# Layer 0 mixer: y projection and memory keys dealt over twelve steps of the dilated attention

## What is computed

```python
def lru_dilated_mixer(h, cos, sin, w_in, conv_w, conv_b, wa, ba, wx, bx, lam, w_out):
    proj = h @ w_in
    x_br, y_br, q, k, v = jnp.split(proj, list(AB_SPLITS), axis=-1)
    rec = rg_lru(causal_depthwise_conv(x_br, conv_w, conv_b), wa, ba, wx, bx, lam) * jax.nn.gelu(y_br)
    q = partial_rope(heads(q), cos, sin)
    k = partial_rope(heads(k), cos, sin)
    att = dilated_attention(q, k, heads(v)).transpose(0, 2, 1, 3).reshape(Bsz, L, B_WIDTH)
    return jnp.concatenate([rec, att], axis=-1) @ w_out
```

## Time and profile before

| | |
|---|---|
| three runs | 1431.32, 1430.82, 1430.17 us (median 1430.82) |
| profiled execution | 1429.49 us; its span in the trace is 1427.3 us, so 2.2 us lie around it |
| PE busy | 1360.2 us of the span (95%) |
| DVE, ACT, POOL busy | 778.0, 344.1, 314.9 us |
| mean granted TensorE clock | 0.979 of full speed |
| from the first y matmul to the first matmul of `xq0` | 156.05 to 336.13 us of the span |

### The profile page before, as it was taken

The page is one execution under the profiler, slowest core; times in us unless marked ns, Lnnn a source line. Parts: engine busy times, 40 slices in busy tenths (PEclk is TensorE's granted clock), DMA queues, the critical chain, the costliest instruction groups (busy, mean ns, idle before and its releaser), DMA issues.

```text
span 1427.3 us, 17280 instructions
## 1 busy us (share of the span) xinstructions
PE 1360.2 (95%) x6344; PEld 1107.2 (78%) x6344; DVE 778.0 (55%) x1159; ACT 344.1 (24%) x715; POOL 314.9 (22%) x358
## 2 busy tenths in 40 slices
PE   8999998899899999999999996799899999999997
PEld 7877785588677888888888884688678888888886
DVE  6997865336556443334436768537475443344434
ACT  4338134212332111001112235513331110001113
POOL 2221224221311121121212125312321212121120
PEclk9999999999999999999999998899999999999998
DMA  5322221023322322233232320022123332323221
GB/s 196 112 89 82 83 96 50 30 89 103 104 74 89 103 90 102 94 98 101 91 103 89 105 88 30 1 87 90 59 89 97 95 103 89 103 89 103 92 99 74
DMA packets 90241, 127.16 MB, mean 89 GB/s; under 512 B 5440, under 2 KB 53824, under 8 KB 90176
## 3 DMA queue, kind: packets, MB, share of 16 engines
q1 hardware_dynamic: 90176, 126.27, 27.6%
HBM read 124.15 MB, written 2.10 MB: 88 GB/s over the span
## 4 chain that ended last, share of the span: by engine, by line
PE 74%; DVE 14%; issue 5%; POOL 3%; DMA 2%; ACT 1%; SPq 0%; DVEq 0%; POOLq 0%; ACTq 0%
PE ps L489 23%; PE ps L493 23%; PE ps L492 23%; DVE w_lo L869 2%; PE ps L593 2%; DVE prob_attn L985 2%; DVE xc L1094 1%; POOL w_hi L452 1%; PE ps L627 1%; POOL prob_attn L444 1%; PE ps L610 1%; DVE acc L890 1%; DVE h L909 1%; POOL prob_xattn L444 1%; DMA raw<-in_xa_wkv 1%
## 5 line engine op out<-in xcount | busy, mean ns | idle before, releaser
L869 DVE TENSOR_TENSOR w_lo<-raw,w_hi 128x1024 fp32r<-128x1024 f32 x226 | 279.4, 1237 | 478.2 <-POOL w_hi L452 476.0
L452 POOL TENSOR_SCALAR w_hi<-raw 128x1024 fp32r<-128x1024 f32 x226 | 252.4, 1117 | 974.6 <-DMA raw<-in_w_gate_up 409.9
L489 PE MATMUL ps<-z_hi,w_hi 128*128 128x512 f32 x1040 | 408.7, 393 | 9.6 <-DVE w_lo L869 3.4
L492 PE MATMUL ps<-z_lo,w_hi 128*128 128x512 f32 x1040 | 405.3, 390 | 0.0
L493 PE MATMUL ps<-z_hi,w_lo 128*128 128x512 f32 x1040 | 405.3, 390 | 0.0
L489 PE MATMUL ps<-f_hi,w_hi 128*128 128x512 f32 x608 | 239.6, 394 | 0.9 <-issue 0.9
L493 PE MATMUL ps<-f_hi,w_lo 128*128 128x512 f32 x608 | 237.1, 390 | 0.0
L492 PE MATMUL ps<-f_lo,w_hi 128*128 128x512 f32 x608 | 237.0, 390 | 0.0
L489 PEld LDWEIGHTS ps<-z_hi,w_hi 128*128 128x128 f32 x1040 | 195.5, 188 | 53.4 <-DVE w_lo L869 4.2
L492 PEld LDWEIGHTS ps<-z_lo,w_hi 128*128 128x128 f32 x1040 | 195.7, 188 | 41.7 <-issue 1.4
L493 PEld LDWEIGHTS ps<-z_hi,w_lo 128*128 128x128 f32 x1040 | 195.6, 188 | 41.0
(11 more groups left out here) (188 smaller groups left out, 1194.5 us busy)
## 6 DMA issues: line engine op xcount, KB each, us to landing
raw<-in_w_gate_up SPq DMA_DIRECT2D x176, 256.0 KB
raw<-in_w_down SPq DMA_DIRECT2D x44, 512.0 KB
raw<-in_w_in SPq DMA_DIRECT2D x28, 512.0 KB
raw<-in_w_out SPq DMA_DIRECT2D x20, 512.0 KB
raw<-in_xa_wkv SPq DMA_DIRECT2D x16, 512.0 KB
raw<-in_xa_wq SPq DMA_DIRECT2D x8, 512.0 KB
raw<-in_xa_wo SPq DMA_DIRECT2D x8, 512.0 KB
raw<-in_w_qkv SPq DMA_DIRECT2D x8, 512.0 KB
```

Source lines behind the costliest of these rows:

```text
L452: pool.tensor_scalar(w_hi[:, slot], raw[:, slot], 1.0, 1.0, ALU.mult, ALU.mult).then_inc(s_hi, 1)
L489: ins = pe.matmul(o, whi, rhi, start=start, stop=False)
L492: pe.matmul(o, whi, rlo, start=False, stop=False)
L869: dve.tensor_tensor(w_lo[:, slot], raw[:, slot], w_hi[:, slot].bitcast(F32), ALU.subtract).then_inc(s_lo, 1)
```

## The change

The stages `in_y` and `attn0` become one stage `mixer` of twelve steps. A step s takes a third of one head pair: the scores of both heads of pair s // 3 for the blocks (128 and 256), 384 or 512 columns. Behind them on PE stands one unit of weights: a half of a pair of y tiles (`y_half`, steps 0 to 7), the memory keys (steps 8 to 11), and from step 12 on a unit of `out0`. The transposes run four steps behind the scores, two thirds of a head at a time, the products with v at steps 7, 10, 13 and 16. The y weights come as units of 512 rows by 256 columns. The scores of both heads of a pair use rows 0 to 63 and 64 to 127 of the array, alternating. `y_in` has two tiles in another place, probabilities and their transposes live where `lru_r`, `lru_a` and z were, the row order of `out0` is 4, 0, 1, 2, 3, 5 (in units of 256 rows; 4 and 5 hold the attention's output), and on DVE `qk_tile(6)` moves ahead of a `low_to`.

```diff
-          ("in_v", 1, 4), ("in_y", 2, 4), ("attn0", 2, 2), ("out0", 2, 6)]
+          ("in_v", 1, 4), ("mixer", 2, 6), ("out0", 2, 6)]
+OUT0_ROWS = (4, 0, 1, 2, 3, 5)
+STEPS, Y_UNITS = 12, 8
...
+        def turns_of(s):
+            if 4 <= s < STEPS + 4:
+                return [((s - 4) // 3, *divmod(k, 3)) for k in (2 * ((s - 4) % 3), 2 * ((s - 4) % 3) + 1)]
+            return []
+        def output_of(s):
+            return (s - 7) // 3 if 7 <= s < STEPS + 7 and s % 3 == 1 else None
...
# POOL
+            high(at_unit, first + 2)
+            for s in range(STEPS + 2):
+                if s % 3 == 0 and s:
+                    normalise_pair(s // 3 - 1)
+                high(first + s + 2, first + s + 3)
...
# PE
+            def mixer_scores(s):
+                p, c = divmod(s, 3)
+                if c == 0:
+                    pe.wait_ge(s_q0, 5 + p)
+                if s:
+                    pe.wait_ge(mx["s_max"], 2 * s)
+                for i in mx["chunks"][c]:
+                    c0 = mx["start"][i] - mx["base"][c]
+                    for e in range(2):
+                        r = slice(HD * e, HD * e + HD)
+                        ins = pe.matmul(ps[:, mx["s_banks"][e], c0:c0 + P * (i + 1)], q0[r, p, i * P:(i + 1) * P],
+                                        k0[r, p, 0:P * (i + 1)], start=True, stop=True)
...
+            def y_half(i):
+                u, t, j = UNIT0["mixer"] + i, i // 2, i % 2
+                pe.wait_ge(s_lo, u + 1)
+                for m in range(2):
+                    if j == 0 and t:
+                        pe.wait_ge(s_y, 2 * t - 1 + m)
...
+            for s in range(STEPS + 5):
+                if output_of(s) is not None:
+                    mixer_values(output_of(s))
+                for item in turns_of(s):
+                    mixer_turns(*item)
+                if s < STEPS:
+                    mixer_scores(s)
+                if s < Y_UNITS:
+                    y_half(s)
+                elif s < STEPS:
+                    if s == Y_UNITS:
+                        pe.wait_ge(s_y, DB)
+                    memory_keys(0, (s - Y_UNITS,))
+                else:
+                    out0_unit(s - STEPS)
+            stage(*out0, first=5)
...
# DVE
+            low_to(gates0 + 13)
+            qk_tile(6)
             low_to(gates0 + 14)
-            qk_tile(6)
             qk_tile(7)
...
+            low_to(mx_unit + 3)
+            for s in range(STEPS + 6):
+                if s in (2, 4, 6, 8):
+                    y_tile(s - 1)
+                for p, e, c in turns_of(s):
+                    if c == 0:
+                        mixer_copied(p, e, c)
+                if s < STEPS:
+                    mixer_maxima(s)
+                if s % 3 == 0 and 0 < s <= STEPS:
+                    mixer_denominator(s // 3 - 1)
+                if s == STEPS:
...
+                if output_of(s - 1) is not None:
+                    mixer_output(output_of(s - 1))
+                if s in (2, 4, 6, 8):
+                    rec(s - 2)
+                    rec(s - 1)
+                if s in (STEPS, STEPS + 1):
+                    for m in range(4 * (s - STEPS), 4 * (s - STEPS) + 4):
+                        rec_low(m)
+                if s < STEPS + 2:
+                    low_to(mx_unit + s + 3)
+                if s in (1, 3, 5, 7):
+                    y_tile(s - 1)
+            dve.wait_ge(mx["s_o_lo"], 4)
+            dve.nop().then_inc(s_free[(GROUP0["mixer"] + 1) % 2], 4)
             residual("xa0", s_done["out0"], group0=GROUP0["out0"], units=(UNIT0["out0"] + 6, UNIT0["xq0"]))
...
# ACT
+            for s in range(STEPS + 5):
...
+                if s < STEPS:
+                    mixer_exps(s)
+                if s in (2, 4, 6, 8):
+                    gelu(s - 2)
+                    gelu(s - 1)
+                if s == STEPS:
+                    act.wait_ge(mx["s_turned"], 18)
+                    for m in range(DB):
+                        rec_high(m)
```

More of the change, by code:

```diff
@@ L119, in attention_plan, with mixer_plan @@
                     values=[(j, P * n, P * i, P, n == 0) for n, (i, j) in enumerate(blocks)])
[L120 to L127, removed]
+    raise ValueError(kind)
+def mixer_plan():
+    chunks = ((0, 1), (2,), (3,))
+    start = [P * i * (i + 1) // 2 for i in range(TB)]
+    blocks = [[(i, j, start[i] + P * j) for i in c for j in range(i + 1)] for c in chunks]
+    return dict(chunks=chunks, start=start, base=[start[c[0]] for c in chunks], blocks=blocks,
+                c_wide=[P * len(b) for b in blocks], width=10 * P)
 def trunk(nc, x, mem, w_in, w_gates, w_out0, w_qkv, w_out1, xa_wq, xa_wkv, xa_wo, w_gate_up, w_down,
@@ L282, in trunk @@
         ATTN = {}
-        for name, heads, plan, tiles in (("attn0", B_HEADS, "attn0", 4), ("xattn0", XH, "xattn", 4),
+        for name, heads, plan, tiles in (("xattn0", XH, "xattn", 4),
                                          ("attn1", C_HEADS, "attn1", 8), ("xattn1", XH, "xattn", 4)):
@@ L361, in rows, with stream @@
                 return w[r0:r0 + 2 * P, bass.ds(col, n)].rearrange("(a p) n -> p a n", p=P)
-            def stream(name, w, units, col0=0, first=0, count=None):
+            def stream(name, w, units, col0=0, first=0, count=None, order=None):
                 n = GROUPS[name] if count is None else count
@@ L370, in body @@
                     for j in range(units):
-                        unit(u0 + units * i + j, [(0, 512, rows(w, 2 * P * j, (first + i) * 512 + col0))])
+                        unit(u0 + units * i + j, [(0, 512, rows(w, 2 * P * (order[j] if order else j), (first + i) * 512 + col0))])
                     seen[0] = keep + units
@@ L1180, in _ @@
                 recur(m)
+            low_to(gates0 + 13)
+            qk_tile(6)
             low_to(gates0 + 14)
-            qk_tile(6)
             qk_tile(7)
-            y0_unit = UNIT0["in_y"]
-            low_to(y0_unit + 6)
-            for m in range(4):
-                y_tile(m)
-            low_to(y0_unit + 7)
-            for m in range(4):
-                rec(m)
-                if m:
-                    rec_low(m - 1)
-            rec_low(3)
-            low_to(y0_unit + 10)
-            for m in range(4, DB):
-                y_tile(m)
@@ L1197, in _, with mixer_maxima @@
-            dve.wait_ge(s_mask0, 16)
-            attention(ATTN["attn0"], {0: lambda: [rec(m) for m in range(4, DB)],
-                                      1: lambda: [rec_low(m) for m in range(4, DB)]})
+            mx_unit = UNIT0["mixer"]
+            low_to(mx_unit + 3)
+            dve.wait_ge(s_mask0, 16)
+            def mixer_maxima(s):
+                p, c = divmod(s, 3)
+                if p == 2 and c == 0:
+                    dve.wait_ge(mx["s_turned"], 6)
+                for e in range(2):
+                    dve.wait_ge(mx["s_scores"], 2 * s + e + 1)
+                    for i in mx["chunks"][c]:
+                        s0, w, c0 = mx["start"][i], P * (i + 1), mx["start"][i] - mx["base"][c]
+                        ins = dve.tensor_tensor_reduce(mx["prob"][2 * p + e][:, s0:s0 + w],
+                                                       ps[:, mx["s_banks"][e], c0:c0 + w], m0[:, TB * P - w:TB * P],
+                                                       -HD ** -0.5, -NEG, ALU.add, ALU.min,
+                                                       stat0[:, p % 3, 1, TB * e + i:TB * e + i + 1])
+                    ins.then_inc(mx["s_max"], 1)
```

210 lines of the change are left out of this document (159 added, 51 removed).

## The result

The changed kernel takes 1421.36 us (median of four runs, 1420.20 to 1424.17), against 1431.07 for four runs of before: ratio 0.9935, 95% interval 0.9918 to 0.9952. That is 9.7 us faster, about twice the forecast's 5 and inside its range. Timed again in more rounds (e12), it is 7.1 us: 1422.35 against 1429.40, ratio 0.9951 (0.9937 to 0.9964).

A forecast was written before the change was run, and what follows sets the result against it. PE bounds the kernel, busy for 1360.2 of 1427.3 us. Work of 150.9, waits of 17.9 and lost clock of 6.6 us end the stretch at 331.5 instead of 336.1, 4.6 less: 1426.0 us expected, range 1418 to 1435.

The forecast's parts named there:

- the waits near 162 and 191: PE waiting for DVE at the second scores, 8.8 us, and at a y matmul (y half 4), 3.0 us.
- the stretch: From the first y matmul to the first matmul of `xq0`, 180.1 us before; forecast 4.6 us less.
- Scores: Attention scores of eight heads, 18.8 us before, 10.0 when paired on the array's two halves: gain 8.8.
- PE's own work: Sum of scores, transposes, values, memory keys, y and `out0` units in the stretch, without any wait: 150.9 us.
- the mild rival: Waits 2 to 4 shrink and only the first clock fall happens: stretch ends at 325, 11 us less; chance 23%.
- wait 3: At step 10, transposes of pair 2 wait 1.4 us for POOL's chain and a copy another 0.5: 1.9 us.
- The clock: Work lost to PE's lower clock in the stretch: three falls, 3.0 and twice about 1.8, together 6.6 us.
- wait 2: At y half 4, PE waits 3.0 us for y tile 2, behind POOL's normalisation and a `w_lo`; one clock fall.
- Costed at nothing: Items given no cost, such as nine table loads instead of two, 9.0 more us of ACT, mostly behind y halves.
- the rival in which a switch holds ACT for 2.7 us: Table loads and gelus come later than walked, 2.7 us per switch instead of 1.28: +2.8 us, 1429; chance 10%.
- The slower case: The clock falls behind all five waits at the highest price, 16.7 us instead of 6.6: 1436.3; chance 15%.
- the halves do not overlap: Paired scores in short chunks keep 1.84 ns a column: 5 us more, 1431; chance 7%.

The follow-up runs named there:

- e12: The changed kernel, unchanged, timed in more rounds beside the kernel before: 1422.35 us against 1429.40, ratio 0.9951.
- e11: e8 with the scores of both heads of a pair on the same half of the array: 1411.20 us, ratio to before 0.9891.
- e8: The changed kernel with the edits of e2, e3 and e7 together: 1403.46 us, ratio to before 0.9836.
- e7: The changed kernel with the reciprocal of a pair's row sums issued on DVE in the pair's third step: 1417.77 us, ratio to before 0.9912.
- e6: The kernel before with only `qk_tile(6)` moved ahead of a `low_to` on DVE: 1429.24 us, ratio to before 0.9993.
- e5: The changed kernel with ACT's gelu replaced by a plain copy, so eight table loads go: 1419.74 us, ratio to before 0.9928.
- e9: The kernel before, unchanged, profiled in another execution: 1426.04 us (one run).
- e3: The changed kernel with `w_lo` of the fifth and sixth `out0` units made ahead of the last output split: 1418.04 us, ratio to before 0.9920.
- e1: The changed kernel with the scores of both heads of a pair on the same half of the array: 1426.31 us, ratio to before 0.9978.
- e4: The changed kernel with POOL making `w_hi` of the next unit ahead of each pair's normalisation: 1420.31 us, ratio to before 0.9933.
- e2: The changed kernel with the last two key-tile rotations moved later on DVE, first maxima right behind the recurrence: 1415.21 us, ratio to before 0.9896.
- e10: The changed kernel, unchanged, profiled in another execution: 1423.05 us (one run).

## Why the prediction was right in its mechanism and off in its size

The median of 1421.36 lies in the range of 1418 to 1435, but 0.6 under the forecast's own 1422 to 1430; e12's 1422.35 lies just inside that. Of the signs that the prediction named, the waits near 162 and 191, the one for `w_lo`, the prices of the scores and a clock of 0.96 are there; the idle time of 15.7 us is just under its 16 to 20, and `xq0` began at 326.1, not 328 to 335, since the stretch itself began 2.5 us earlier.

The stretch was forecast 4.6 us shorter and is 7.4 shorter between the first two profiled executions; with the others of both kernels it is 179.8 before (mean of 180.1 and 179.4) and 173.1 after (172.6, 173.3 and 173.4), 6.7 less. By the terms of the sum, for the first two:

- **Scores.** That the pairing is what shortens PE's work is shown: it is worth 8.4 in e11 against e8. Against the 18.8 that eight heads cost before, the pairs cost 11.1, not 10.0, so it is 7.7 and not 8.8: the chunks with their hand-overs take 1.08 ns a column, where the estimate had 0.98.
- **PE's own work.** Forecast 150.9, measured 153.3 in e8, where hardly a wait and no fall of the clock is in the way. From start to start in its trace: scores 11.1, y 45.2 (44.2), transposes 9.5, values 9.3 (9.6), memory keys 12.0, `out0` 66.2 (65.6). So the sum was 2.4 us short: 1.1 in the scores, and 0.11 at each of the y and `out0` units that now stand behind small matmuls. I took these matmuls' price from a place where nothing interrupts them.
- **The waits.** Four of the five were where the walk put them, the third a step later; 15.7 us instead of 17.9. The mis-sized ones are 2 and 3, each some 0.7 to 1.1 too long: the mild rival was right on these in kind. Of wait 3 the larger part, 1.4 at step 10 for POOL's normalisation, isn't there; what is there is the copy, which the walk had at 0.5 and which took 0.8. The chain behind it is the walked one: in e7, with the reciprocal made earlier, it went.
- **The clock.** This is the term that was most wrong: 3.6 us instead of 6.6. I had counted a fall behind every wait of 2.7 us or more, and wait 2 as one of 3.0. It was 2.3, and the clock stayed at 1.00; the fall behind the first wait cost 1.9, not 3.0. The prices of 3.0 and more came from places where PE worked through the whole fall (224 to 231 and 840 to 846 us); here 6.4 us and more of it lay over a PE that stood idle anyway.
- **Together**: -2.2 (waits), -3.0 (clock), +2.4 (work) make -2.8 on the stretch, which is 4.6 against 7.4. Two errors to one side and one to the other: the forecast stood closer than its terms, and that is luck.
- **Against before.** Without waits and lost clock the stretch holds 153.3 us of work instead of 159.2 (180.1 - 13.8 - 7.1): 5.9 less, of which the scores are 7.7 less and the rest 1.8 more, mostly the changes from small matmuls to units. The waits took 1.9 back (13.8 to 15.7), and the lost clock fell from 7.1 to 3.6, 3.5 less, where the forecast had 0.5. So the deeper waits took back less than the half of the pairing's gain that the forecast gave them (1.9 us, not 4.1), and nearly half of the 7.4 is clock. This is also the term that varies most: with before's waits, e6 lost more to it than before did.
- **Costed at nothing.** The table loads were worth about 1 us (e5), so the rival in which a switch holds ACT for 2.7 us falls. ACT's timeline of the changed kernel has a load, two gelus and a load back to back, with 0.01 to 0.02 us between them:

```profile
180.36 1.28 ACT L1692 ACT_TABLE_LOAD   x1
181.65 1.15 ACT L1692 ACTIVATE y_in<-y_in 128x512 f32<-128x512 f32 x2
182.82 1.28 ACT L1704 ACT_TABLE_LOAD   x1
```

  The Trainium skill's page "ScalarE: Activation LUTs", section "What ACT_TABLE_LOAD costs", counts about 2.66 us for each switch; these rows disagree, also where switches follow each other closely.

- **The rivals.** The mild case (325 for the end, -11) was close in its sums, 15 of waits and 3 of clock against 15.7 and 3.6, though two falls came and not one; the work that it shared with the forecast was 2.4 short. Its reason, that PE at the lower clock gives DVE and POOL time, no run tests. The slower case needed falls of 11.2 us; with five waits there were two. That the halves do not overlap is refuted by e11.
- **Outside the stretch.** The forecast said that nothing changes. In three executions of before's order (one of them e6) 1090.9 to 1091.4 us follow `xq0`'s first matmul, in the three of the changed kernel 1092.3 to 1092.5. The change gives about 1 us back there. In the window from 550 to 650 us behind that matmul, around layer 1's attention, the clock is 0.91 in all three of after and 0.94, 0.96 and 0.94 in before, e9 and e6. Whether that is the change's doing stays open: e3 and e5 had 1091.1 and 1091.6, and e1, e7 and e8 had 0.94 in that window and still 1092.3 to 1093.5, so the window alone doesn't explain it.

So the traces bear out 5 to 7 us, and e12's 7.1 (interval 5.1 to 9.0) agrees with them. The rest of the first comparison's 9.7 is put down to the spread of the runs, since e12 doesn't repeat it.

## What to carry to other kernels

When work is interleaved in finer steps, walk the queue of each helping engine from the first step on. The finer steps were not what cost time here: the helpers' items stood in an order that was fit for the old steps, and reordering the same items (DVE as busy as before) was worth 18 us, 2.5 times the change itself. Put what the next step of the critical engine needs ahead of what is needed three steps later, and where a queue is late as a whole, look for the input that comes late (e7) and don't swap its items (e4).

Undo one wait at a time to learn its price, but expect a part of it to come up at the next (e2: 8.2 us of wait and 1.9 of clock removed at the first scores, 6.0 gained, since the next wait grew by 1.0 and had a fall behind it), and try the edits together: three that shortened the stretch by 6.0, 4.4 and 4.7 us apart shortened it by 18.2 together, 3 more than their sum, in part because in e2 alone a wait and a fall had come up that e7's edit takes away.

A term of a floor ("PE's work without a wait") is best read from rows that stand in the same surroundings as the new ones: a unit of matmuls behind another unit is cheaper than one behind small matmuls.

## What the runs showed of the hardware that wasn't expected

**The same wait has a fall of the clock behind it in one execution, and none in the next.** In all of these programs PE waits for ACT near 110 us. Here are the waiting matmul in the timeline and the window of 112 to 116 us, in before, in e9 (the same kernel) and in e6:

```profile
110.77 0.50 PE L489 MATMUL ps<-z_hi,w_hi 128*128 128x512 f32 x1 [1.92 <-ACTq L1481]
...
112.00:116.00 4.00, 4.00 (x12) 3.09 (x11) 3.56 (x8) 3.97 (x9) 0.98 (x1) 0.57 0.44 131
```

```profile
109.94 0.50 PE L489 MATMUL ps<-z_hi,w_hi 128*128 128x512 f32 x1 [2.20 <-ACTq L1481]
...
112.00:116.00 4.00, 4.00 (x20) 3.30 (x19) 3.43 (x9) 3.97 (x7) 1.06 (x1) 1.00 0.31 111
```

```profile
110.18 0.50 PE L489 MATMUL ps<-z_hi,w_hi 128*128 128x512 f32 x1 [1.77 <-ACTq L1481]
...
112.00:116.00 4.00, 4.00 (x20) 3.30 (x19) 3.56 (x9) 3.97 (x8) 1.05 (x1) 1.00 0.37 127
```

The shorter wait had the fall and the longer one had none. The last wait of the changed kernel (2.79 us, the same to the hundredth each time) had one in after, e2, e4, e10 and e12, and none in e1, e5 and e7. e5 had one behind its 2.2 us wait for `y_in`, where the changed kernel had none in three executions. So 1.6 to 1.9 us of a stretch, 0.1% of this kernel, hang on something that the length of the wait doesn't decide, and a single profile can't tell an edit's effect of that size; the number of waits in the trace can.

**POOL and DVE are slower side by side.** The `w_lo` in the second wait's chain took 2.05 us while POOL made two `w_hi`, instead of the 1.2 of its neighbours. In e7 the first pair's normalisation took 6.02 us on POOL, with DVE busy for 3.9 us of it; in the changed kernel it took 4.12, with DVE idle throughout. The changed kernel's last one took 6.01 beside 4.0 us of DVE's work. What they contend for no run here shows.
